# One expert call in place of two in layer 0 of a two-block network: three token tiles dense, the fourth by gathered rows

## The reference, cut to what matters

```python
def _peer(h, wq, keys, u, v):
    q = (hb @ wq).reshape(tc, PEER_HEADS, 2, PEER_HALF)
    ...
    # top 16 of 128 keys twice per head, top 16 of their sums, softmax over the 16
    # out = sum over the 128 chosen e of  share[e] * gelu(h . u[e]) * v[e]
```

## Time and profile before

| | us |
|---|---|
| median of 3 runs (range) | 4061.45 (4057.35 to 4062.14) |
| profiled execution: span from first to last instruction | 4058.2 |
| PE busy | 3915.4 (96%) |
| DVE busy | 3021.8 (74%) |
| ACT busy | 1831.6 (45%) |
| POOL busy | 6.5 (18 instructions) |
| mean granted TensorE clock | 0.987 of 2.4 GHz |

### The profile page before, as it was taken

How to read it: one execution, slowest core, us unless ns; L and a number is a source line. 1 busy time by engine, 2 the same in 40 slices (tenths; PEclk the granted TensorE clock), 3 DMA queues, 4 the chain that set the end, 5 groups by cost and what they waited for, 6 DMA issues and landing times. The chain is left out here.

```text
span 4058.2 us, 66160 instructions
## 1 busy us (share of the span) xinstructions
PE 3915.4 (96%) x25874; PEld 3500.9 (86%) x25874; DVE 3021.8 (74%) x6784; ACT 1831.6 (45%) x2929; POOL 6.5 (0%) x18
## 2 busy tenths in 40 slices
PE   7999999999999999999999899999999799998999
PEld 6768999988889999988887699999888688988798
DVE  4557797788886877788984579777888767766875
ACT  3344444443334444433444344444333535555454
POOL 0000000000000000000000000000000000000000
PEclk8999999999999999999999999999999899999999
DMA  5144575566667865567751357655666422442243
GB/s 218 60 162 152 191 227 176 169 203 239 244 228 271 315 232 169 169 237 254 258 205 57 121 169 232 193 169 182 243 244 244 158 86 91 178 175 104 78 167 146
DMA packets 121829, 752.17 MB, mean 185 GB/s; under 512 B 15728, under 2 KB 17265, under 8 KB 57265
## 3 DMA queue, kind: packets, MB, share of 16 engines
q1 hardware_dynamic: 121520, 747.93, 52.5%
HBM read 693.88 MB, written 54.00 MB: 184 GB/s over the span
## 5 line engine op out<-in xcount | busy, mean ns | idle before, releaser
L1922 DVE TENSOR_TENSOR expert_ring_low<-expert_ring,expert_high 128x1024 fp32r<-128x1024 f32 x768 | 935.6, 1219 | 248.0 <-ACT expert_high L2192 247.7
L2192 ACT ACTIVATE expert_high<-expert_ring 128x1024 fp32r<-128x1024 f32 x768 | 811.8, 1057 | 619.0 <-PE ps L2119 616.0
L2088 PE MATMUL ps<-peer_hT_high_peer,expert_high 128*128 128x256 f32 x3072 | 882.3, 287 | 1.2 <-DVE expert_ring_low L1922 1.0
L2089 PE MATMUL ps<-peer_hT_low,expert_high 128*128 128x256 f32 x3072 | 861.0, 280 | 0.0
L2090 PE MATMUL ps<-peer_hT_high_peer,expert_ring_low 128*128 128x256 f32 x3072 | 861.0, 280 | 0.0
L2088 PEld LDWEIGHTS ps<-peer_hT_high_peer,expert_high 128*128 128x128 f32 x3072 | 583.2, 190 | 3.3 <-DVE expert_ring_low L1922 2.4
L2089 PEld LDWEIGHTS ps<-peer_hT_low,expert_high 128*128 128x128 f32 x3072 | 584.0, 190 | 0.0
L2090 PEld LDWEIGHTS ps<-peer_hT_high_peer,expert_ring_low 128*128 128x128 f32 x3072 | 578.9, 188 | 0.0
L2119 PE MATMUL ps<-expert_high,weighted_high 128*128 128x512 f32 x1536 | 474.9, 390 | 7.4 <-DVE weighted_low L1952 7.4
L2119 PE MATMUL ps<-expert_high,weighted_low 128*128 128x512 f32 x1536 | 473.8, 390 | 0.0
L2119 PE MATMUL ps<-expert_ring_low,weighted_high 128*128 128x512 f32 x1536 | 473.4, 389 | 0.0
(11 more groups left out here) (720 smaller groups left out, 6924.3 us busy)
## 6 DMA issues: line engine op xcount, KB each, us to landing
expert_ring<-in_peer_u SPq DMA_DIRECT2D x192, 1024.0 KB, 5.2
expert_ring<-in_peer_v SPq DMA_DIRECT2D x192, 1024.0 KB, 4.9
gelu_peer<-gelu_out SPq DMA_DIRECT2D x186, 256.0 KB, 5.5
gelu_in_peer<-gelu_peer SPq DMA_DIRECT2D x93, 512.0 KB, 5.7
weight_ring<-in_ffn_w_up SPq DMA_DIRECT2D x22, 2048.0 KB, 7.3
weight_ring<-in_w_in SPq DMA_DIRECT2D x14, 2048.0 KB, 7.4
weight_ring<-in_w_mod SPq DMA_DIRECT2D x12, 2048.0 KB, 8.1
weight_ring<-in_peer_wq SPq DMA_DIRECT2D x12, 2048.0 KB, 7.3
```

What stands on the lines that cost most here:

```text
L1922: dve.tensor_tensor(piece(low, n), piece(raw, n), high[:, n % LEAD, :].bitcast(F32), ALU.subtract).then_inc(low_done, 1)
L2088: pe.matmul(o, b[:, s], hT_h[:, c, :], start=(c == 0), stop=False)
L2089: pe.matmul(o, b[:, s], hT_l[:, c, :], start=False, stop=False)
L2192: act.activation(high[:, n % LEAD, :], piece(raw, n), ACT.Identity).then_inc(high_done, 1)
```

## The change: what it does

The two layer-0 calls become one, `first_experts`.

- `mix_queries` makes the queries of all four tiles: 8 groups (unit, half of the tokens) of 4 in place of 4, and turns the second half of the hidden rows between them.
- The expert stage goes over the 128 rows once. Tiles 0, 1 and 2 are dense (`DT = 3`, `DW = 384` columns): 24 matmuls of 384 columns per row in the U half, 3 x 3 x 2 = 18 matmuls of 512 columns in the V half. The table of weights is made for 384 tokens, from row 32 on, goes to DRAM and comes back in pieces. Its one-hots are one DVE instruction for four tokens (`equal`), the share is multiplied in on ACT (`shares`).
- Tile 3 is sparse (`SPARSE`). For each of its 128 pairs GpSimd gathers 128 rows of U (one row of 4 KB for each token) and 128 rows of V by an indirect DMA, DVE makes the 128 dots (`sparse`, one instruction of 128x1024 with a sum), ACT applies gelu to eight at a time (`gates`), and GpSimd multiplies the V rows by the coefficient and adds them to the sum (`add`).
- `select` runs over four tiles in the order 0, 3, 1, 2 and then `sparse` follows in the same generator. The budgets per row are `EARLY_NS` 2600 (rows 0 to 30), `TABLE_NS` 2300 (rows 31 to 127) and `DOWN_NS` 1700 (V half).
- `gla_front` now does the layernorm of all four tiles, both turns and the low parts of the next mixer's first two weight units (on GpSimd), and nothing of it is done beside the V half.

The core of the diff:

```diff
-        peer(nc, G, 0, 0, [0, 1], None, mixed)
-        peer(nc, G, 0, 1, [2, 3], LateModulation(G, 1, 12, G.mod_next))
+        first_experts(nc, G, mixed, LateModulation(G, 1, 12, G.mod_next))
...
+DT = 3
+DW = DT * P
+TILES = (0, 3, 1, 2)
+SPARSE = 3
+TABLES_AT = 32
+TABLES = DW // TOKS
+PART = 8
+LAG = PART + 2
+U_SLOTS, V_SLOTS = 3, 4
+ADD_LAG = 2
+EARLY_NS, TABLE_NS, DOWN_NS = 2600, 2300, 1700
...
+class ExpertsVector(Experts):
+    def sparse(self, dve, step):
+        G, S, B, at = self.G, self.S, self.B, self.at
+        dve.wait_ge(S.h_kept, 2)
+        dve.wait_ge(S.mod_out, 1)
+        step.wait()
+        for n in range(PAIRS):
+            s, (k, m) = n % U_SLOTS, divmod(n, PART)
+            u = G.x[:, s, :]
+            if m == 0 and k >= 3:
+                dve.wait_ge(S.gated, k - 2)
+            dve.wait_ge(G.u_landed[s], 16 * (n // U_SLOTS + 1))
+            dve.scalar_tensor_tensor(u, u, 1.0, B.h_rows[:, :], ALU.mult, ALU.mult,
+                                     accum_out=B.dots[:, k % 3, m:m + 1]).then_inc(S.dotted, 1)
+            if m == PART - 1:
+                at[f"part{k}"] = at["now"]
+            yield 1250
+    def equal(self, dve, g):
...
+        dve.tensor_tensor(B.eq[:, g % 2, :, :, :], G.iota[:, :].unsqueeze(1).unsqueeze(1).broadcast_to([P, 2, TOKS, P]),
+                          B.table[:, 0:2, g * TOKS:(g + 1) * TOKS].unsqueeze(3).broadcast_to([P, 2, TOKS, P]),
+                          ALU.is_equal).then_inc(S.eq_ready, 1)
+    def run(self, dve):
...
+        pieces, left = chain(self.select(dve, step), self.sparse(dve, step)), 0
+        for r in range(N_KEYS):
+            at["now"] = r
+            if r < N_KEYS - 1:
+                self.split_low(dve, r + LEAD)
+            if 0 <= r + 1 - TABLES_AT < TABLES:
+                self.equal(dve, r + 1 - TABLES_AT)
+            left += EARLY_NS if r < TABLES_AT - 1 else TABLE_NS
+            while left > 0:
+                left -= next(pieces, left)
...
+        for r in range(N_KEYS):
+            at["now"] = N_KEYS + r
+            if r + 2 < N_KEYS:
+                self.split_weights(dve, r + 2)
+            if r + 3 < N_KEYS:
+                self.weigh(dve, r + 3)
+            if N_KEYS + r + LEAD < N:
+                self.split_low(dve, N_KEYS + r + LEAD)
+            left += DOWN_NS
+            while left > 0:
+                left -= next(pieces, left)
...
+class ExpertsTensor(Experts):
+    def products_u(self, pe, r):
...
+        for c in range(DC):
+            s = slice(c * P, (c + 1) * P)
+            pe.matmul(o, b[:, s], B.hs[0][:, c, 0:DW], start=(c == 0), stop=False)
+            pe.matmul(o, b[:, s], B.hs[1][:, c, 0:DW], start=False, stop=False)
+            mm = pe.matmul(o, lo[:, s], B.hs[0][:, c, 0:DW], start=False, stop=(c == DC - 1))
+    def products_v(self, pe, r):
...
+        for t in range(DT):
+            for x, y in PASSES:
+                for h in range(2):
+                    mm = pe.matmul(G.ps[:, 2 * t + h, :], (B.ah, B.al)[x][:, r % 3, t * P:(t + 1) * P],
+                                   v[y][:, h * 512:(h + 1) * 512], ...)
...
+class ExpertsPool(Experts):
+    def run(self, pool):
+        G, S, B = self.G, self.S, self.B
+        pool.wait_ge(S.spots_ready, 1)
+        pool.wait_ge(S.mod_out, 1)
+        pool.wait_ge(S.table_ready, 1)
+        for n in range(PAIRS + LAG + ADD_LAG):
+            if n < PAIRS:
+                if n >= U_SLOTS:
+                    pool.wait_ge(S.dotted, n - U_SLOTS + 1)
+                pool.indirect_dma_start(G.x[:, n % U_SLOTS, :], None, B.rows_u,
+                                        bass.IndirectOffsetOnAxis(B.spots[:, n:n + 1], 0)).then_inc(...)
+            if LAG <= n < PAIRS + LAG:
+                m = n - LAG
+                if m >= V_SLOTS:
+                    pool.wait_ge(S.summed, m - V_SLOTS + 1)
+                pool.indirect_dma_start(B.v_rows[:, m % V_SLOTS, :], None, B.rows_v,
+                                        bass.IndirectOffsetOnAxis(B.spots[:, m:m + 1], 0)).then_inc(...)
+            if n >= LAG + ADD_LAG:
+                self.add(pool, n - LAG - ADD_LAG)
+    def add(self, pool, n):
...
+        pool.tensor_scalar(v, v, c, None, ALU.mult).then_inc(S.scaled, 1)
+        pool.wait_ge(S.scaled, n)
+        pool.wait_ge(S.summed, n)
+        pool.tensor_tensor(y, y, v, ALU.add).then_inc(S.summed, 1)
...
 def gla_front(nc, G, F, B, u0):
...
+            gated(0)
+            gated(1)
             first(0)
             first(1)
-            for q in (2, 3):
...
             second(0)
             second(1)
+            dve.wait_ge(x_normed, 2)
+            gated(2)
+            gated(3)
+            for q in range(QUARTERS):
+                hidden_low(0, q)
+            first(2)
+            first(3)
+            second(2)
+            second(3)
```

More of the change, by code:

```diff
@@ L2 @@
 from contextlib import ExitStack, contextmanager
-from itertools import count, product
+from itertools import chain, count, product
 import concourse.bass as bass
@@ L2602, in product @@
                 mm.then_inc(F.q_ready, 1)
[L2604 to L2625, removed]
+        pe.wait_ge(F.f_whole, DC)
@@ new lines, in products @@
+        for q in range(QUARTERS):
+            pe.wait_ge(F.q_low, q + 1)
+            pe.wait_ge(F.f_low, q + 1)
+            for k in range(4):
+                for c in (2 * q, 2 * q + 1):
+                    product(k, c)
+        for m, (i, part) in enumerate(self.ORDER):
+            if m == 0:
+                continue
+            if m == 1:
+                pe.wait_ge(F.y_used, 8)
+            if m == 2:
+                pe.wait_ge(F.f_low, 2 * QUARTERS)
+            for k in range(4 * m, 4 * m + 4):
+                if k == 6:
+                    pe.wait_ge(F.v_out, 2)
+                    pe.wait_ge(F.s_out, 2)
+                    pe.wait_ge(F.normed, 2 * PT)
+                    for q in range(QUARTERS):
+                        self.turn_quarter(pe, 1, q)
+                if k >= 8:
+                    pe.wait_ge((F.v_out, F.s_out)[k % 2], k // 2 - 3)
+                for c in range(DC):
+                    if part == 0 and k == 4 * m and c % 2 == 0:
+                        pe.wait_ge(F.q_low, QUARTERS * i + c // 2 + 1)
+                    product(k, c)
+            if part == 1:
+                ws.done(self.units[i], F.q_ready, 4 * (m + 1))
@@ L2630, in rest_scalar @@
             self.part_high(act, 1, q)
[L2631 to L2639, removed]
+        self.out_s(act, (1, 3))
@@ L3172, in _, with turn @@
-            for q in range(QUARTERS):
+            def turn(part, q):
                 for c in (2 * q, 2 * q + 1):
@@ new lines, in _ @@
+            for q in range(QUARTERS):
+                act.activation(F.q.high[:, 2 * q:2 * q + 2, :], F.q.raw[:, 2 * q:2 * q + 2, :], ACT.Identity).then_inc(q_high, 1)
+            std(0)
+            std(1)
+            hidden(0)
+            act.wait_ge(k_landed, 16)
+            for q in range(QUARTERS):
+                act.activation(F.k.high[:, 2 * q:2 * q + 2, :], F.k.raw[:, 2 * q:2 * q + 2, :], ACT.Identity).then_inc(k_high, 1)
+            std(2)
+            std(3)
+            for h in range(H_C):
+                query_out(h)
```

805 lines of the change are left out of this document (705 added, 100 removed).

## The result

The changed kernel takes **4370.3 us** (median of 4 runs, 4368.5 to 4371.6) where the kernel before took 4061.8 beside it: ratio 1.0762, 95% interval 1.0746 to 1.0777. The forecast was 4005 in a range of 3800 to 4215. It is slower by 308 us, 155 us beyond the upper end.

What follows compares the result with a forecast made beforehand. PE's own work, busy 99%, was taken to bound the kernel before. PE terms of -392 us plus a 335 us stall at GpSimd's pace gave -57, from 4058.2 or 4061.45 to a stated 4005; range 3800 to 4215.

Steps and rivals of the forecast that it cites:

- U half: First half of the expert rows on PE: 676 us in place of 906.6, so -231.
- V half: Second half of the expert rows on PE: 529 us in place of 710.6, so -182.
- P: Pace of a dot, GpSimd's whole work per sparse pair (two gathers, scaling, add): 5.8 us, floor 2.8, ceiling 14.8.
- The form of the sum: Stall of PE on the sparse tile added to the dense terms: -392 + 335 = -57 us.
- The stall: PE's wait on sparse dots: 34 us for the first 12 pairs + 116 x P - 372, 335 at 5.8.
- The break-even point: Value of P at which the change gains nothing: 6.3 us.
- The dense part: PE's terms for queries, both halves and the stage after, without any wait: +1 - 231 - 182 + 20 = -392 us.
- Queries: Query stages on PE merged into one: second stage's -58.7 us gone, its matmuls and other work added, together +1.
- Stage after: After the V half, norms lose their cover: end at some 45 us in place of 24.8, +20.
- the selection's end at row 82: DVE's selection takes 199.3 us of budget and ends at row 82; only then come the dots.
- Rival B: Slower: VectorE and GpSimd stand in each other's way, P 7.2, stall 497, +105, 4166 us; chance 0.38.

Runs made afterwards that it cites:

- experiment 1: Changed kernel without tile 3's experts (no gathers, dots, gates or weighted sums; GpSimd only zeroes the sum once): 3745.0 us, ratio 0.922 to the kernel before.
- experiment 7: Changed kernel with GpSimd's scaling of V rows as `tensor_tensor` with a broadcast coefficient in place of `tensor_scalar`: 4342.5 us, ratio 1.0687.
- experiment 4: Changed kernel with the weighted sum moved to VectorE as one `scalar_tensor_tensor` per pair, GpSimd only issuing gathers: 3791.8 us, ratio 0.933.
- experiment 10: experiment 4 with SP's reload of x issued at row 124 of the V half, ahead of that row's refill: 3779.1 us, ratio 0.931.

## Why the prediction was wrong

**The step that failed is the price of GpSimd's turn**, P = 5.8, and in it above all `tensor_scalar`: "A memset of 128x1024, one stream, takes 0.95. `tensor_scalar` has two streams: 0.95 to 1.9; I take the middle, 1.4." It takes 2.91, half again the stated ceiling. Counting streams does not give the price here: `tensor_scalar` has fewer than the sum's `tensor_tensor` and is slower. The other terms were off less, and all to the same side:

| a pair, us | forecast | measured |
|---|---|---|
| `tensor_scalar` | 1.4 | 2.91 |
| `tensor_tensor` | 2.1 | 2.51 |
| two issues | 2.1 | 1.42 + 1.14 |
| waits, gaps | 0.2 | 0.60 |
| P | 5.8 | 8.59 |

The gaps are 8.59 less the four means (7.99). The largest of them, 0.3 ahead of every V gather, stands in the groups above as idle time until "issue". The gaps add up over GpSimd's timeline as well: 0.31, 0.15, 0.08 and 0.04 ahead of its four kinds of work. The estimate from the Trainium skill (GPSIMD Engine Reference, Performance versus the Vector engine: 4497 ns for an add of 2048 elements; half of it, an estimate, is 2.25 for 1024) is close to what the sum takes with VectorE idle, 2.38 (below). It was nearer than the 2.1 that the sum went by.

**The form of the sum held.** The stall was to be 34 + 116 x P - PE's need for those rows. That need is 391 with experiment 1's rates (46 x 5.59 + 32.4 x 4.13; 372 in the forecast). Against the span of experiment 1:

| | P | sum | measured |
|---|---|---|---|
| changed kernel | 8.59 | 639 | 626 |
| scaling as `tensor_tensor` | 8.14 | 587 | 602 |
| no scaling | 6.09 | 349 | 350 |

Three kernels with P from 6.1 to 8.6 lie within 15 us of it. P is taken from the same runs here, so this tests the form of the sum, not the forecast of P: beyond GpSimd's pace little is missing from it. That experiment 7 lies 15 us above it fits its slower rows after the last dot (26 us more than in the changed kernel). The break-even point, put at 6.3, is in truth P = (4061 - 3745 + 391 - 34) / 116 = 5.8. So the forecast P would have given no change, not a gain of 57: the rest of the sum was too low as well.

**The dense part was 74 us too cheap** (span 3740.2 for 4058.2 - 392 = 3666.2):
- Queries: the U half starts at 487.6, forecast 433.6 + 58.7 + 1 = 493.3. Better by 6.
- U half: 731 for 676. The pace of 384 columns is right (0.174 for 0.172). But a table row is 5.59 for 5.21, 36 us in 96 rows: an undisturbed one takes 5.51, of which the group of four tokens is 5.51 - 24 x 0.174 = 1.33 and not the 1.08 of the calls before (why is open: the order of the two operands is the same); the rest are six waits for ACT's scaling. And 17 us are the handover to the V half, the table's way through DRAM, which was costed at nothing (28 us in the changed kernel).
- V half: 528 for 529. Right. Whether VectorE's 4.04 fits into a row's 4.08 these rows don't say, since after the dots it has only 53% of them to fill (122.65 of 230.7 us from 2140 on). In experiment 4, where it carries dots and sums (busy 479 of 554 us), this half takes 26 us more.
- Stage after: +45 in the place of +20. VectorE's first norm step starts 17 us after the last V product, where the forecast had it at once; 12 of them are the reload of x (experiment 10). "GpSimd's splits of the weight units lie beside this" was not free either: the norm step of 1.28 in the earlier trace rows takes 3.25 beside them.

In sum the forecast span of 4001 was missed by 365 us: 2.79 x 116 = 323 for P, 74 for the dense part, -19 since PE's rows in the stall take 391 for 372, and -13 that the sum leaves over.

**What held.** One dot after another at GpSimd's pace; the selection's end at row 82 (first dot at 959.2, behind the 86th `split_low`, which runs three rows ahead); PE at half its time in between; V rows of 4.08 after the dots; the granted clock below full there (0.74). That it has no large price of its own is argued: PE is idle half of this time, and the sum above has no term for it and leaves 13 us over the other way.

**Rival B was half right.** It said slower, by VectorE and GpSimd excluding each other, P 7.2 and 4166. Exclusion there is, and the Trainium skill's rule (SBUF: State Buffer, section SBUF: two separate sides) is borne out for GpSimd's `tensor_tensor`: a Vector instruction with two SBUF inputs and a GpSimd one that reads SBUF exclude each other. For `tensor_scalar` it is not, or only in part. Here are seven consecutive instructions of GpSimd in the changed kernel, in time order:

```profile
1308.00 2.34 POOL L3435 TENSOR_TENSOR x<-x,chosen_v 128x1024 f32<-128x1024 f32 x1
1310.49 1.82 POOL L3405 DMA_INDIRECT x<-in_peer_rows,spots  x1 [0.15 <-POOL x L3435]
1312.61 1.90 POOL L3411 DMA_INDIRECT chosen_v<-in_peer_v,spots  x1 [0.31 <-issue]
1314.55 2.86 POOL L3432 TENSOR_SCALAR chosen_v<-chosen_v,coefs 128x1024 f32<-128x1024 f32 x1
1317.50 2.37 POOL L3435 TENSOR_TENSOR x<-x,chosen_v 128x1024 f32<-128x1024 f32 x1
1320.02 1.01 POOL L3405 DMA_INDIRECT x<-in_peer_rows,spots  x1 [0.15 <-POOL x L3435]
1321.34 0.94 POOL L3411 DMA_INDIRECT chosen_v<-in_peer_v,spots  x1 [0.30 <-issue]
```

and VectorE's in the same stretch:

```profile
1308.20 3.22 DVE L3010 SCALAR_TENSOR_TENSOR x<-x,hidden_rows 128x1024 f32<-128x1024 f32 x1 [8.62 <-DMA x<-in_peer_rows,spots]
1311.35 1.22 DVE L2908 TENSOR_TENSOR expert_ring_low<-expert_ring,expert_high 128x1024 fp32r<-128x1024 f32 x1
1312.49 1.21 DVE L3022 TENSOR_TENSOR equal<-iota,pair_table 128x1024 f32<-128x1024 f32 x1
1315.57 1.23 DVE L3010 SCALAR_TENSOR_TENSOR x<-x,hidden_rows 128x1024 f32<-128x1024 f32 x1 [1.86 <-DMA x<-in_peer_rows,spots]
```

The dot at 1308.20 starts with GpSimd's sum at 1308.00, and is over 2.0 later than alone; the sum takes its usual 2.34. The dot at 1315.57 lies wholly inside a `tensor_scalar`, and neither is longer: this form doesn't exclude the dot. And the issues at 1310.49 and 1312.61 are 0.8 and 1.0 longer than those at 1320.02 and 1321.34, with VectorE busy beside the first pair and idle beside the second. Counted over the timeline from 1000 to 1600: GpSimd's `tensor_scalar` is 2.86 with VectorE idle (16 of them) and beside it (54); the sum 2.38 (12) and 2.54 (58, up to 3.38); the U issue 1.01 (28) and 1.81 (42); the V issue 0.94 (57) and 1.69 (13).

In the V half a `tensor_scalar` does have a price. VectorE's `weighted` (128x384, 0.56 alone) takes 1.18 inside this one, which is itself 0.46 longer than alone:

```profile
1985.94 3.32 POOL L3432 TENSOR_SCALAR chosen_v<-chosen_v,coefs 128x1024 f32<-128x1024 f32 x1
1986.74 1.18 DVE L3040 TENSOR_TENSOR weighted<-gelu_in,pair_weights_in 128x384 f32<-128x384 f32 x1
```

Twelve of them with `split_low`, `weighted` and `weighted_low` beside them take 3.26 in the mean. What tells `weighted` from the dot was not tried.

What this costs P is the means less the values with VectorE idle: 0.41 and 0.20 for the issues (1.01 and 0.94 alone), 0.13 for the sum, 0.05 for the scaling, 0.8 in all, or 92 us. By this estimate the kernel would still stand near 4278 without it. So GpSimd's own price alone makes the change slower, and the exclusion adds to it. That the longer VectorE instructions fall mostly into VectorE's idle time is argued, not tried.

It also explains experiment 7, by argument and by its tail above: `tensor_tensor` for `tensor_scalar` buys 1 us of GpSimd's time with a form that VectorE has to share.

## What to carry to other kernels

When a change puts elementwise work on GpSimd in a row-by-row pipeline, sum up all that GpSimd does for one step, issues and gaps too, and hold it against the pace the other engines need (here 2.9 us against 8.6). With no row of that operation, don't take a ceiling from a memset: a `tensor_scalar` cost three of them here. A fused instruction on VectorE (1.28 us) can be cheaper than two on GpSimd (5.4) even where VectorE looks full, since what VectorE lost here was waiting. And for every buffer that now goes through DRAM, or that is lent to another use, find the one transfer between its last writer and its first reader: two such holes of 17 us, of which the one at x could be cut to 6, stood outside all the per-row sums.

## What the runs showed of the hardware that was not expected

- On GpSimd, `tensor_scalar` of 128x1024 float32 takes 2.81 us with a constant and 2.92 with a pointer; `tensor_tensor` takes 1.94 with one operand broadcast and 2.34 at least with two full ones.
- Beside GpSimd's `tensor_tensor`, VectorE's two-input 1.22 us become up to 3.4. Beside its `tensor_scalar` the dot stays at 1.23 and the `tensor_scalar` at 2.86; but VectorE's `weighted` of 128x384 goes from 0.56 to 1.18 in the V half, and the `tensor_scalar` to 3.32.
- An indirect issue of 128 rows of 4 KB holds GpSimd for 0.94 to 1.01 us with VectorE idle. Beside a busy VectorE it took 1.8 in the mean for the U issue in the table rows and 1.3 in the V half, and up to 1.9; a further 0.3 us stands ahead of the second of two in a row.
